# Layer 0's convolution, norms, rotation and differential attention behind the pieces of its projection, and the last norm in rows by tokens

## What is computed

```
h  = rms_norm(x, g) * (1 + scale) + shift          # shift, scale, gates from silu(c) @ ada_w ("ada")
qa, ka, va, qkv_b, g_b, gates_b = split(h @ w_in)   # and the same for the context
# differential attention, 4 heads, two maps of 64 features each
q1, q2, k1, k2 = rms_norm over each 64 features, times gain; latent tokens rotated (rope)
p = softmax(q1 k1' / 8) - lam * softmax(q2 k2' / 8)
a = rms_norm(p @ v, subln) * (1 - lam_init)
# gated delta rule, 4 heads of 128 features
y = silu(conv over 5 tokens of qkv_b);  q, k = l2_norm;  beta, log_alpha from gates_b
b = rms_norm(chunked delta rule, forwards and backwards) * silu(g_b)
x = x + gate * ([a, b] @ w_out);  then a SwiGLU feed-forward with 2816 hidden features
...
return rms_norm(h, final_norm)[:, 16:]              # after the last layer of the second block
```

## Time and profile before

| | us |
|---|---|
| median of 3 runs | 4213.74 (4205.14 to 4214.31) |
| the profiled execution, own time | 4210.84 |
| its span, first to last instruction | 4209.0 |
| TensorE (PE) busy | 3689.8 (88%) |
| VectorE (DVE) busy | 1565.3 (37%) |
| ScalarE (ACT) busy | 1296.9 (31%) |
| GpSimd (POOL) busy | 1095.2 (26%) |
| mean granted TensorE clock | 0.939 of 2.4 GHz |

### The profile page before, as it was taken

How to read it: one execution, slowest core, us unless ns; L and a number is a source line. 1 busy time by engine, 2 the same in 40 slices (tenths; PEclk the granted TensorE clock), 3 DMA queues, 4 the chain that set the end, 5 groups by cost and what they waited for, 6 DMA issues and landing times.

```text
span 4209.0 us, 60584 instructions
## 1 busy us (share of the span) xinstructions
PE 3689.8 (88%) x24406; PEld 3248.4 (77%) x24406; DVE 1565.3 (37%) x2369; ACT 1296.9 (31%) x1836; POOL 1095.2 (26%) x447
## 2 busy tenths in 40 slices
PE   6994925887789999989989998988999989989997
PEld 4782724887668888878867786977899978779997
DVE  2117576444332122065533232454322235433132
ACT  3111443333231111145535222344432233434121
POOL 1220002332112222211123443212343322124342
PEclk9996967999899999989999999999999999999999
DMA  5330000000134112101112222111222211112221
GB/s 202 150 134 5 1 12 1 1 1 11 40 120 156 58 55 72 48 26 44 42 62 70 94 96 69 66 41 47 71 90 87 92 50 56 41 55 90 85 93 61
DMA packets 61954, 273.13 MB, mean 65 GB/s; under 512 B 6689, under 2 KB 7728, under 8 KB 58608
## 3 DMA queue, kind: packets, MB, share of 16 engines
q1 hardware_dynamic: 61072, 268.05, 18.0%
q0 software_dynamic: 736, 3.00, 0.2%
HBM read 268.92 MB, written 2.10 MB: 64 GB/s over the span
## 4 chain that ended last, share of the span: by engine, by line
PE 81%; DVE 11%; ACT 5%; issue 2%; DMA 1%; DVEq 0%; POOL 0%; SPq 0%; ACTq 0%; POOLq 0%
PE ps L342 50%; PE ps L1798 7%; PE ps L1489 4%; DVE scr L661 3%; PE ps L574 2%; PE ps L1260 2%; PE ps L1265 1%; PE ps L710 1%; DVE scr L964 1%; PE ps L894 1%; PE ps L1524 1%; PE ps L1534 1%; PE ps L694 1%; ACT nscr L565 1%; DVE nscr L581 1%
## 5 line engine op out<-in xcount | busy, mean ns | idle before, releaser
L330 POOL TENSOR_TENSOR w_lo<-raw,w_hi 128x1024 fp32r<-128x1024 f32 (+1 forms) x380 | 970.2, 2554 | 2399.3 <-ACT w_hi L302 2399.3
L302 ACT CAST w_hi<-raw 128x1024 fp32r<-128x1024 f32 (+1 forms) x380 | 419.9, 1105 | 1785.4 <-PE ps L342 1594.8
L342 PE MATMUL ps<-act_hi,w_hi 128*128 128x264 f32 (+3 forms) x3360 | 839.2, 321 | 100.4 <-DVE act_lo L589 47.2
L342 PE MATMUL ps<-act_lo,w_hi 128*128 128x264 f32 (+3 forms) x3360 | 830.9, 319 | 0.0
L342 PE MATMUL ps<-act_hi,w_lo 128*128 128x264 f32 (+3 forms) x3360 | 830.3, 319 | 0.0
L342 PEld LDWEIGHTS ps<-act_hi,w_hi 128*128 128x128 f32 x3360 | 576.5, 190 | 172.1 <-issue 111.5
L342 PEld LDWEIGHTS ps<-act_hi,w_lo 128*128 128x128 f32 x3360 | 581.2, 190 | 43.9
L342 PEld LDWEIGHTS ps<-act_lo,w_hi 128*128 128x128 f32 x3360 | 581.7, 190 | 42.0
L519 DVE TENSOR_TENSOR nscr<-nscr,ps 128x264 f32<-128x264 f32 (+2 forms) x154 | 71.4, 499 | 773.5 <-PE ps L342 773.5
L342 PE MATMUL ps<-ff_hi,w_hi 128*128 128x264 f32 (+2 forms) x1232 | 307.2, 320 | 45.0 <-DVE ff_lo L524 45.0
L342 PE MATMUL ps<-ff_lo,w_hi 128*128 128x264 f32 (+2 forms) x1232 | 306.3, 319 | 0.0
(11 more groups left out here) (348 smaller groups left out, 4963.7 us busy)
## 6 DMA issues: line engine op xcount, KB each, us to landing
raw<-in_gu SPq DMA_DIRECT2D x176, 512.0 KB, 3.4
arena<-in_ada SPq DMA_DIRECT2D x24, 2048.0 KB, 7.9
raw<-in_dn SPq DMA_DIRECT2D x64, 704.0 KB, 4.0
raw<-in_in SPq DMA_DIRECT2D x56, 512.0 KB, 3.4
raw<-in_even_in SPq DMA_DIRECT2D x28, 512.0 KB, 3.5
raw<-in_odd_in SPq DMA_DIRECT2D x24, 512.0 KB, 3.4
raw<-in_out SPq DMA_DIRECT2D x16, 512.0 KB, 3.5
raw<-in_even_out SPq DMA_DIRECT2D x8, 512.0 KB, 3.5
```

What stands on the lines that cost most here:

```text
L302: act.copy(w_hi[:, j, 0:cols], raw[:, j, 0:cols]).then_inc(s["hi_ready"], 1)
L330: pool.tensor_tensor(w_lo[:, j, 0:cols], raw[:, j, 0:cols], w_hi[:, j, 0:cols].bitcast(F32), ALU.subtract).then_inc(s["lo_ready"], 1)
L342: mm = pe.matmul(ps[:, 2 * j + b, 0:cn], wt[:, j, w], acts[:, k, c0:c0 + cn], start=(k == 0 and wt is w_hi and acts is hi), stop=(k == kt ...
```

## The change

Layer 0's stages 2 to 6, up to the delta rule's tables, become one stage, `front`, and one short `gates_tab`:

- The projection goes by items, 28 blocks in two halves (256 and 512 columns, one PSUM bank each, 56 items). The blocks come in a new order: 12 of the delta rule's q, k, v; then q, k, v of each attention head; then its 4 gate blocks.
- Behind the items, in orders written out by hand: the gate logits (behind items 1 and 3), the convolution of a block as soon as it is there, the norms of the delta rule's q and k (events 6 to 21, finished one item later), q's and k's preparation for each head from item 24 on, the transposition of v, and one attention unit behind each item from 31 to 54. The output's norm of a head comes 11 items and more after its first unit.
- q is no longer divided by its root; the root enters the scale of the exponential (`q_scale`). Scores are copied negated out of PSUM with a running minimum, in a piece of 256 and one of 512 columns for each map; VectorE combines the two maps, and TensorE transposes the result plainly (6 matmuls for 768 keys instead of diagonal products of 12). There is one PSUM bank for outputs and transposed parts together, so that a turn waits for the copy of the output before (`diff_taken`).
- Six ada groups are done in `front` instead of eleven; the feed-forward of layer 0 takes nine behind its first half, as before, and five behind its second.
- The last norm transposes the residual first; ScalarE squares 1024 columns of each row with an accumulator, VectorE multiplies by root's reciprocal and a row of gains in one instruction, and each of the four token tiles is stored by a DMA of its own.
- All constants are loaded from ScalarE's queue. GpSimd's DMA scratch shrinks, and buffers move in SBUF.

The core of the diff:

```diff
-        ADA_BEHIND = dict(even_in=(3, 1, 12), gu0=(14, 1, 10))
-        ADA_TURNS = dict(first=(3, 1, 4), second=(7, 0, 8), ffn=(14, 1, 10))
+        ADA_FRONT = (3, 1, 7)
+        ADA_TURNS = ((9, 1, 10), (19, 0, 5))
...
+        def pe_front(pe, n):
...
+            def turn(u):
+                _, _, nk = diff_unit(u)
+                pe.wait_ge(s["diff_p"], u + 1)
+                if u:
+                    pe.wait_ge(s["diff_copied"], u)
+                    pe.wait_ge(s["diff_taken"], u)
+                for t in range(nk // P):
+                    mm = pe.transpose(ps[:, 5 + t // 4, (t % 4) * P:(t % 4 + 1) * P], dz[:, u % 2, 0, t * P:(t + 1) * P], ident)
+                mm.then_inc(s["diff_turned"], 1)
...
+            for at in range(ITEMSF):
+                item(at)
+                if at == 1:
+                    gate_logits()
+                if at == 3:
+                    gate_turn()
+                if at % 2 and ADA_FRONT[1] <= at // 4 < ADA_FRONT[2]:
+                    pe_ada_behind(pe, ADA_FRONT[0] + at // 4, (at % 4) // 2)
...
+                if front_event(at):
+                    event(*front_event(at))
+                if at >= 31:
+                    u = at - 31
+                    if u:
+                        turn(u - 1)
+                    if u < UNITSF:
+                        scores(u)
+                    if u:
+                        weigh(u - 1)
+                if sub_event(at) is not None:
+                    event("sub", sub_event(at))
...
+        def act_front(act, n):
...
+            for at in range(ITEMSF):
+                if at % 2:
+                    act.wait_ge(s["front_done"], at + 1)
+                    act_split(act, (at // 2) % 2, 16 * (at // 4 + 2), ahead[at // 4])
...
+                if front_event(at) and front_event(at)[0] != "turn":
+                    root(*front_event(at))
...
+                if at % 4 == 1 and 5 <= at <= 25:
+                    for m in (at // 2 - 2, at // 2 - 1):
+                        convert(m)
+                    for m in (at // 2 - 2, at // 2 - 1):
+                        if m < 8:
+                            square_converted(m)
+                if at % 2 and at < 24:
+                    first_tap(at // 2)
+                if at >= 31:
+                    u = at - 31
+                    if u:
+                        copy(u - 1)
+                    if u < UNITSF:
+                        exp(u)
...
+        def dve_front(dve, n):
...
+            def shift(u):
...
+                for m in range(2):
+                    ins = dve.tensor_scalar(dz[:, u % 2, m, 0:CTX], ps[:, 4, CTX * m:CTX * m + CTX], -1.0, None, ALU.mult, ALU.min,
+                                            accum_out=small[:, 8 + m:9 + m])
...
+                        ins = dve.tensor_tensor_reduce(dz[:, u % 2, m, CTX:T], ps[:, 2 + m, 0:LAT], none.to_broadcast([P, LAT]), -1.0,
+                                                       small[:, 8 + m:9 + m], ALU.add, ALU.min, small[:, 10 + m:11 + m])
...
+            def combine(u):
...
+                dve_link(dve, n, dve.tensor_scalar(z1, z1, both, None, ALU.mult))
+                dve.scalar_tensor_tensor(z0, z0, inv[:, 0:1], z1, ALU.mult, ALU.add).then_inc(s["diff_p"], 1)
...
+            for at in range(ITEMSF):
+                evict(at)
...
+                if at >= 31 and at - 31 < UNITSF:
+                    shift(at - 31)
+                if late and late[0] != "turn":
+                    finish(*late)
+                if sub_event(at - 1) is not None:
+                    finish("sub", sub_event(at - 1))
+                if at >= 31 and at - 31 < UNITSF:
+                    combine(at - 31)
+                if at >= 32:
+                    take(at - 32)
+                if 26 <= at < 48 and (at - 26) % 6 == 0:
+                    rope("dq", (at - 26) // 6)
+                if 29 <= at < 48 and (at - 29) % 6 == 0:
+                    rope("dk", (at - 29) // 6)
+                if at % 2 == 0 and 2 <= at <= 24:
+                    convolve(at // 2 - 1)
...
+        def act_final(act, n):
+            for t in range(4):
+                act.wait_ge(s["final_ready"], t + 1)
+                act_link(act, n, act.activation(row_squares, ps[:, 2 * t:2 * t + 2, :].rearrange("p a t -> p (a t)"), ACT.Square,
+                                                accum_out=small[:, 40 + t:41 + t]))
...
-            project(BOTH, 4, lambda m, b: qk[:, m, BOTH[b][0]:BOTH[b][0] + BOTH[b][1]], ada="first")
-            project(BOTH, 8, lambda m, b: gd[:, m, (2, 260)[b]:(2, 260)[b] + BOTH[b][1]], ada="second")
-            project_tok(TILES, 2, v0)
...
+            stage("front", {})
```

More of the change, by code:

```diff
@@ L355, in turn @@
                     pe_products(pe, j, hi, lo, halves, kt, first if j == 0 else None)
-                    if g0 is not None:
-                        pe_ada_behind(pe, i + g0, j)
-            for a, b, g0 in stretches(turns, ada):
-                if a == 0 and fresh is not None:
-                    turn(0, g0, fresh)
-                    a = 1
-                if a < b:
-                    each(pe, a, b, lambda i: turn(i, g0))
+            if fresh is not None:
+                turn(0, fresh)
+            with pe.Fori(0 if fresh is None else 1, turns) as i:
+                turn(i)
         def pe_gate_up(pe, n, halves, ada=None):
```

877 lines of the change are left out of this document (452 added, 425 removed).

## The result

The changed kernel takes 4037.9 us (median of 4 runs, 4030.9 to 4040.4) against 4211.6 us (4 runs, 4205.1 to 4214.3): a ratio of 0.9587, 95% interval 0.957 to 0.9604. The forecast was 4021 us, range 3975 to 4080. The profiled execution has a span of 4038.6 us (own time 4040.4, clock 0.954; before 0.939), 170.4 us less than the 4209.0 before, where the working had 190.

A forecast was written before the change was run, and what follows sets the result against it. Bound: a VectorE stage, an attention and a VectorE stage in series (344 us) after a projection leaving VectorE idle. 183 + 3 - 13 - 2 + 19 = 190 us off 4210.8 gives 4021 us, range 3975 to 4080.

The forecast's parts named there:

- (a): Items 0 to 5 of the new stage, with the gate logits and one ada part: item 6 starts at 103 us.
- (b): Items 6 to 23: nine blocks bounded by VectorE, 12.7 us each including 1.2 us stall, 114 us; item 24 starts at 217.
- (c): Items 24 to 31, four blocks: TensorE takes 39.5 us, VectorE fits with 27; item 31 ends at 257 us.
- (d): The 24 attention units: 220 us plus 8 for hand-overs and half-clock stretches, 228 us; the stage reaches 485 us.
- (e): Last output norm in series behind the units: about 8 us; end at 494 us instead of 677, 183 us saved.
- The tables of functions: ScalarE's table switches in the stage, 1.28 us each, costed at nothing; by the skill page up to some 20 us more.
- The ada groups: Five groups moved into layer 0's second feed-forward half, where TensorE is full: 2.6 us each, 13 us added.
- signs of being wrong: In the stage: convolution stalls on ScalarE's Silus, clock leaves 1.0 for whole heads, or a unit takes other than 9-10 us.
- all hidden: TensorE never waits for a unit or VectorE: stage ends at 432 us instead of 494, kernel 3959 us; chance 0.15.
- A longer way: Port stalls, table loads and half clock add up in the units: up to 4134 us, likely about 4070; chance 0.20.
- Slower: Gaps keep TensorE at 1.2 GHz through the stage, which ends at 789 us; kernel 4316 us; chance 0.02.
- it does not do what it says: Items run after VectorE's work, not beside it: 77 + 103 us more, stage ends at 674, kernel 4201 us; chance 0.03.

The follow-up runs named there:

- the control: The changed kernel run once more without edits: 4034.4 us, against 4208.3 us for the kernel before.
- the three edits of the units: On the changed kernel: output copy before combination, map 0's shift before map 1's minima, 8 added matmuls per gap; with front subtraction in four and ada in front 4014.2 us.
- the last kernel: The changed kernel with five edits together, GpSimd's subtraction in four instructions in every stage: 3980.9 us, ratio 0.9458 to the kernel before.

## Why the prediction was right, and where its steps were off

The verdict and the mechanism were right: three stages in series became one, TensorE is the engine that is busy, and what it waits for is a unit's way through VectorE. The steps, in their order:

- **(a)** Item 6 at 103 us: item 6 is evicted at 108.3, so it started near 105. 2 us off.
- **(b)** 12.7 us a block, item 24 starting at 217. It started at 216.2, but VectorE was not through: the eviction of item 23 came at 222.2, and item 25 waited for it. So (b) and (c) have to be read together, from the start of item 6 to the end of item 31. The forecast was 154 us; it took 157.6, in the control 159.6, with the subtraction cut to an eighth 144.5 and in four 145.5. Without the stall the forecast would have been 143.5 (9 x 11.5 + 40), so all of it but the stall was right to 1 us, and the term that was too small is the size of the stall. I took half of one subtraction, 1.2 us a block or 11 us; it cost 13 to 15 us, 1.5 to 1.7 a block, between the ends 0 and 2.4. The taps alone lost 13.7 us over twelve blocks and 15.9 in the control, with 2.1 in a block that meets a whole instruction, as at 160.9 us; the scalings of 256 columns lost 0.2 us each (0.70 for 0.48).
- **(c)** Item 31 at 257 us: evicted at 262.7, 5.7 late. 2 us are (a). The rest is how (b)'s backlog on VectorE came out: item 25 waited 3.6 us for that eviction and then ran at half clock for 5.3 us, so that it took 8.3 us where others take 5.7.

```profile
222.97 0.80 PE L942 MATMUL ps<-act_hi,w_hi 128*128 128x512 f32 x1 [3.62 <-DVE arena L1171]
```

- **(d)** 228 us for the units. From item 31 to the last copy (504.7) it is 242, 14 more. The long unit was right (9.4 to 9.5 us; 9.6), so was the fifth (12.7; 13.1). The heads took 59.6, 58.3, 63.9 and 58.8 us; 54.4, 54.4, 57.4 and 54 were forecast. Three terms were too small. The short units, 5.2 and 8.3, took 7.3 and 9.8 in the second head: I had left out that TensorE weighs the long unit before (1.6 us) in the first, and makes the sums of the next head's rows in it. A head's last unit, 8.6, took 9.3 to 9.7. In the third head an output's norm, a rotation and a collision with GpSimd stand in one window, and the clock falls behind it. Of the 8 us for hand-overs and half-clock stretches the clock took most or all: filling the gaps gave 6.2 us net, and 9.7 in the units where it did not overrun.
- **(e)** A tail of 8 us took 12.0 (504.7 to 516.6): more than one norm is left at the end. Behind the last copy VectorE still has the 512 columns of the third head's output, and then 256 and 512 of the fourth's.
- **The gates' tables:** 3 us saved; measured 2.3.
- **The tables of functions:** costed at nothing, and right: 39 loads of 1.28 us stand in the stage, and the exponentials wait for VectorE's shift in 24 of 24 units. I had weighed that against the Trainium skill, "ScalarE: Activation LUTs", section "What ACT_TABLE_LOAD costs", whose drain of 1.38 us would by my estimate have added up to some 20 us. The trace does not show that drain here either: the square root starts 0.02 us after its load's end (339.75 + 1.28, then 341.05).
- **The ada groups:** +13, measured +15.4. I took 2.6 us from the projection; in the feed-forward a group costs 3.08.
- **The constants' DMAs:** +2, measured nothing.
- **The end:** 19, measured 19.8, and the 14 us between last projection and end are 14.0.

Together, against the 190: 23.3 us less from the stage and its tables, 2.4 less from the feed-forward; 2 more from the DMAs, 0.8 from the end and 3.3 from the drift in between: 170.4.

Of the signs, TensorE is busy for 93% from 70 to 215 us and VectorE for 93% from 105 to 217. The turn waits in 11 of 23 cases, every second as forecast. The delta rule's first matmul stands 24 us behind the 500. Two signs of being wrong need a word. The granted clock is 0.91, 0.94, 0.89 and 0.91 over the four heads, so it leaves 1.0 in every head, in stretches and not throughout. And not every unit takes 9 to 10 us: the long ones mostly take 9.3 to 10.2, but 10.9 and 11.5 in the third and fourth heads, and fifth units take 12.7 to 13.2.

The rivals: "all hidden" is refuted by the 25.6 us of waits before turns, and by a stage that ends 85 us behind its 432. "A longer way" was half true, in the parts that the experiments put a price on: the stall, which I placed on combinations and which falls on taps, small scalings, first shifts and one rotation, and the clock; its table loads did not come. "Slower" is refuted by the clock above. Of "it does not do what it says" a little is there: up to 264 us TensorE waits 7.9 us, in four cases, for evictions that stand behind taps and reciprocals, where that rival had 77.

The experiments also agree with the Trainium skill, "SBUF — State Buffer", section "Who interferes with whom", by which the shared ports are an exclusive lock and whoever issues first has them for the whole instruction. That GpSimd waits as well is likely and not shown: its subtractions of 1024 columns range from 2.34 to 2.98 us in the control, and no run isolates why. If a lock is held for an instruction, it is held for less when the instruction is shorter; the cutting did this, with 12.5 us in the front stage (17 by the trace of the stage) and 33 in the rest.

What stays open, since no kernel was run for it: why the start differs by 3 us between executions, why a feed-forward turn took 16.96 us in two runs, and which waits of the later layers, beside the eight for the last low part, the subtraction in four makes shorter.

## What to carry to other kernels

When three serial stages are folded into one pipeline, its time is the sum of windows, so list for each window what each engine does in it, the leftovers of the unit before included; the long and the fifth units' windows, which I had listed fully, were right to 0.5 us, the short units' were 1.5 to 2 us off. Look for long GpSimd instructions that read SBUF beside a busy VectorE, and cut them before anything else is moved: here that took three lines and gave some 43 us, 10 in the front stage with the chip's difference taken off and 33 in the rest, where the three edits of the units together gave about 9. An addition of 0.15 us in the wrong place of an engine's order cost 48 us (4077.3 against 4026.4, less the chip's 2.9); whenever a step is asked for sooner, look at what is queued ahead of it.

## What was not expected of the hardware

- The cost of a collision between VectorE and GpSimd goes with the length of the instruction that holds the port, not with GpSimd's load. A tap of 1.02 us took up to 3.24 beside instructions of 2.4 us, and up to 1.56 beside instructions of 0.73 us that do the same work. Four short instructions ahead of each long one, twice the work, cost the taps less (60.3 us in all) than the long one alone (65.2). An instruction of two columns, 0.16 us alone, took 2.33 us.
- A cast with a single input from SBUF is hit as well: 128x768 columns took 2.69 us beside a subtraction that had started 0.13 us before it, and 1.02 us beside the same work in four instructions (at 1340.1 us of the last kernel).
- TensorE's clock fell behind gaps of about 4 us between long stretches of full work: turn and scores then ran at half speed (six transposes 1.51 us instead of 0.85), which made the way from turn to shift 1.5 us longer; matmuls without use in the gap prevented it (granted clock of the units 0.97 and not 0.91).
